# The last output projection of an encoder trunk: weight slices and four mixed blocks loaded one block earlier, slice 0 split ahead of the finish, semaphore clearing behind the memsets

## What is computed

```python
def rwkv7_time_mix(...):
    ...
    _, y = lax.scan(step, jnp.zeros((bsz, H, Dh, Dh), F32), xs)
    y = jnp.moveaxis(y, 0, 1)
    mu = jnp.mean(y, axis=-1, keepdims=True)
    var = jnp.mean(jnp.square(y - mu), axis=-1, keepdims=True)
    y = ((y - mu) * lax.rsqrt(var + RWKV_GN_EPS)).reshape(bsz, T, W) * ln_w + ln_b
    bonus = jnp.sum(rh * kh * r_k, axis=-1, keepdims=True) * vh
    return y + bonus.reshape(bsz, T, W)

def odd_layer(...):
    ...
    o_c = g_a * jax.nn.sigmoid(g_b) * jax.nn.silu(z_c.astype(F32))
    ...
    o_d = o_d * jax.nn.silu(z_d.astype(F32))
    mixed = jnp.concatenate([o_c, o_d], axis=-1).astype(x.dtype)
    return x + mixed @ w_out
```

## Time and profile before

| | us |
|---|---|
| median of 3 runs | 1481.3 |
| lowest and highest | 1479.28, 1483.59 |
| the profiled execution | 1474.99 |
| its span, first to last instruction | 1473.2 |

### The profile page before, as it was taken

One profiled execution on the slowest core, in us unless ns is written; L12 is line 12 of the kernel. 1 busy time (PEld: TensorE's weight loads), 2 busy tenths in 40 slices (PEclk: granted clock), 3 DMA queues, 4 the chain that ended last, 5 costly groups with the idle time before them and its releaser, 6 DMA issues. The chain is left out here.

```text
span 1473.2 us, 20646 instructions
## 1 busy us (share of the span) xinstructions
PE 1285.9 (87%) x8498; PEld 1069.1 (73%) x8498; DVE 892.4 (61%) x1191; ACT 481.5 (33%) x823; POOL 306.1 (21%) x156
## 2 busy tenths in 40 slices
PE   4999999979879959987997999999942788899698
PEld 4677888868568947876886888887721677889587
DVE  5267763840067646237978456686969888364831
ACT  5233344321336643223242212225462312222400
POOL 2223221211013346013131112122400400000420
PEclk9999999989989979998999999999965699999899
DMA  5212211320310012431242341621200000000523
GB/s 190 44 44 54 47 44 51 111 87 15 115 50 1 1 67 91 157 86 44 87 118 85 82 107 30 193 58 39 77 15 0 2 1 2 22 37 2 201 85 114
DMA packets 117558, 97.79 MB, mean 66 GB/s; under 512 B 37016, under 2 KB 102680, under 8 KB 117336
## 3 DMA queue, kind: packets, MB, share of 16 engines
q1 hardware_dynamic: 103832, 77.45, 17.7%
q10 hardware_dynamic: 13632, 19.01, 4.0%
HBM read 70.23 MB, written 24.51 MB: 64 GB/s over the span
## 5 line engine op out<-in xcount | busy, mean ns | idle before, releaser
L172 PE MATMUL banks<-xt_lo,w_hi 128*128 128x512 f32 x816 | 323.7, 397 | 5.9 <-POOL w_lo L521 5.9
L173 PE MATMUL banks<-xt_hi,w_lo 128*128 128x512 f32 x816 | 320.1, 392 | 0.0
L174 PE MATMUL banks<-xt_hi,w_hi 128*128 128x512 f32 x816 | 319.9, 392 | 0.0
L521 POOL TENSOR_TENSOR w_lo<-features,w_hi 128x1024 fp32r<-128x1024 f32 x55 | 148.8, 2707 | 524.2 <-ACT w_hi L531 524.2
L172 PEld LDWEIGHTS banks<-xt_lo,w_hi 128*128 128x128 f32 x816 | 154.8, 190 | 41.7 <-POOL w_lo L521 6.2
L174 PEld LDWEIGHTS banks<-xt_hi,w_hi 128*128 128x128 f32 x816 | 154.6, 190 | 32.7
L173 PEld LDWEIGHTS banks<-xt_hi,w_lo 128*128 128x128 f32 x816 | 154.8, 190 | 31.5
L580 ACT ACTIVATE temporaries<-banks 128x1024 f32<-128x1024 f32 x47 | 56.0, 1192 | 328.6 <-PE banks L174 320.7
L172 PE MATMUL banks<-xt_lo,oout_mh 128*128 128x512 f32 x128 | 51.1, 400 | 11.9 <-DVE xt_lo L1609 11.9
L300 PE MATMUL banks<-temporaries,features 128*128 128x128 f32 x256 | 37.8, 311 | 25.9 <-DVE temporaries L277 25.9
L531 ACT ACTIVATE w_hi<-features 128x1024 fp32r<-128x1024 f32 x55 | 57.8, 1054 | 1.6 <-PEq L197 1.0
(11 more groups left out here) (488 smaller groups left out, 2602.0 us busy)
## 6 DMA issues: line engine op xcount, KB each, us to landing
features<-in_even_w_in SPq DMA_DIRECT2D x26, 512.0 KB, 4.0
features<-in_odd_w_in SPq DMA_DIRECT2D x25, 512.0 KB, 4.5
features<-in_x SPq DMA_DIRECT2D x8, 512.0 KB, 8.0
even_gates<-temporaries ACTq DMA_DIRECT2D x8, 512.0 KB, 2.6
features<-even_gates SPq DMA_DIRECT2D x8, 512.0 KB, 8.8
features<-in_even_w_out SPq DMA_DIRECT2D x8, 512.0 KB, 3.5
temporaries<-in_x SPq DMA_DIRECT2D x8, 512.0 KB, 4.5
h_between_layers<-features SPq DMA_DIRECT2D x8, 512.0 KB, 2.9
```

Source lines behind the costliest of these rows:

```text
L172: nc.tensor.matmul(out, w[0], x[1], start=start, stop=False)
L173: nc.tensor.matmul(out, w[1], x[0], start=False, stop=False)
L174: return nc.tensor.matmul(out, w[0], x[0], start=False, stop=stop)
L521: nc.gpsimd.tensor_tensor(wl[n % 2], wr[n % NW], wh[n % 2].bitcast(F32), ALU.subtract).then_inc(low, 1)
```

## The change

Four things are changed, all in the odd layer.

- The loads of the first three weight slices and of S5's four blocks move from the beginning of block 4 to block 3, behind the gate loads in SyncE's queue. S5's blocks get other places in SBUF (`s5_out`), since their old ones are in use in block 3. Two of these places are later written by the high parts `mh[4]`, `mh[5]` and one by the low part of a weight slice; hence the two new waits on `low_m`.
- In block 4 the due numbers of the early slices change: on ScalarE from 5, 7.5, 10, 12.5 to 0, 2.5, 5, 7.2; on GpSimd from 5 + 2.5k to 2.5k; on VectorE from 6, 9.5, 11, 15.5 to -1, 6, 11, 15.5; on PE from 8, 11.5, 15, 18.5 to 1, 6, 9.5, 14. The finish's numbers stay.
- The clearing of blocks 1 to 3 is due at 4 instead of -2.
- `fetch` and its loop are gone from `project_out`; it is given the semaphores `mixed_in` instead.

```diff
@@ project_out
     def scalar(act):
         for k in range(KT):
-            yield 5 + 2.5 * k if k < early else base + k
-            if k < len(fetch):
+            yield (0, 2.5, 5, 7.2)[k] if k < early < KT else base + k
+            if k < len(mixed_in):
                 act.wait_ge(mixed_in[k], 16)
             if k == early:
                 act.wait_ge(*ready)
+                act.wait_ge(low_m, early)
...
     def gpsimd(pool):
         for k in range(KT):
-            yield 5 + 2.5 * k if k < early else base + k
+            yield 2.5 * k if k < early else base + k
...
         for k in range(KT):
-            yield 8 + 3.5 * k if k < early else base + 2 + k
+            yield (1, 6, 9.5, 14)[k] if k < early < KT else base + 2 + k
...
     def vector(dve):
         for k in range(KT):
-            yield (6, 9.5, 11, 15.5)[k] if k < early < KT else base + k
+            yield (-1, 6, 11, 15.5)[k] if k < early < KT else base + k
+            if k == early:
+                dve.wait_ge(low_m, early)
@@ gates_of
+        for to, what, sem in ahead:
+            sp.dma_start(to, what).then_inc(sem, 16)
         sp.wait_ge(gates_in, 16 * 4)
@@ odd_layer
-    side_by_side(co, clearing(co), invert(co, "ri0", first.n_st, R7_INVERT[0]), r7_prepare(co, second, beside_preparation(33)))
-    side_by_side(co, clearing(co), r7_state(co, first), invert(co, "ri1", second.n_st, R7_INVERT[1], pace=lambda t: 1.5 * t))
-    side_by_side(co, clearing(co), gates_of(co, zg), r7_state(co, second), r7_finish(co, first, (co.gates_in, 64), A_BIG, 0, lambda t: 5 + 3.4 * t))
+    side_by_side(co, clearing(co, at=4), invert(co, "ri0", first.n_st, R7_INVERT[0]), r7_prepare(co, second, beside_preparation(33)))
+    side_by_side(co, clearing(co, at=4), r7_state(co, first), invert(co, "ri1", second.n_st, R7_INVERT[1], pace=lambda t: 1.5 * t))
+    w_in, mixed_in = ([co.sem(f"oout_{n}{i}", kept=True) for i in range(count)] for n, count in (("w", 3), ("mixed", WB)))
+    s5_out = [co.at(at, (T,)) for at in (A_F[3], A_F[3] + 1024, A_BIG + 14336, A_BIG + 15360)]
+    loads = [(co.at(A_F[4] + 1024 * i, (D,)), a["odd_w_out"][0][i * P:(i + 1) * P, :], w_in[i]) for i in range(3)]
+    loads = [load for i in range(WB) for load in loads[i:i + 1] + [(s5_out[i], oc[i], mixed_in[i])]]
+    side_by_side(co, clearing(co, at=4), gates_of(co, zg, loads), r7_state(co, second), r7_finish(co, first, (co.gates_in, 64), A_BIG, 0, lambda t: 5 + 3.4 * t))
     side_by_side(co, clearing(co, at=100), r7_finish(co, second, None, A_BIG + 4096, 6, lambda t: t),
-                 project_out(co, "oout", a["odd_w_out"][0], zc + r, [A_F[2] + 1024 * k for k in range(KT)], [A_F[0] + 1024 * k for k in range(KT)], x, dst,
-                             co.output_stored, fetch=[(zc[b], oc[b]) for b in range(WB)], early=WB, ready=(co.finish_done, 2)))
+                 project_out(co, "oout", a["odd_w_out"][0], s5_out + r, [A_F[2] + 1024 * k for k in range(KT)], [A_F[0] + 1024 * k for k in range(KT)], x, dst,
+                             co.output_stored, fetched=w_in, early=WB, ready=(co.finish_done, 2), mixed_in=mixed_in))
```

More of the change, by code:

```diff
@@ L1502, in swa_attend, with project_out @@
     return dict(sync=sync, gpsimd=gpsimd, tensor=tensor, vector=vector, scalar=scalar)
-def project_out(co, tag, w, mixed, hi_at, lo_at, res, dst, stored, fetched=False, fetch=(), early=KT, ready=None, keep=None):
+def project_out(co, tag, w, mixed, hi_at, lo_at, res, dst, stored, fetched=False, early=KT, ready=None, keep=None, mixed_in=()):
     nc = co.nc
@@ L1519, in project_out @@
     resin = [co.sem(f"{tag}_r{i}") for i in range(3)]
-    mixed_in = [co.sem(f"{tag}_mixed_in{i}") for i in range(len(fetch))]
     high_w, high_m, low_w, low_m, multiplied, added = (
@@ L1533, in sync @@
                 sp.dma_start(wr[k], w[k * P:(k + 1) * P, :]).then_inc(loaded[k], 16)
-            if k < len(fetch):
-                sp.dma_start(*fetch[k]).then_inc(mixed_in[k], 16)
-        for k in range(3, len(fetch)):
-            sp.dma_start(*fetch[k]).then_inc(mixed_in[k], 16)
         for k in range(3):
@@ L2604, in r7_state, with gates_of @@
     return dict(gpsimd=gpsimd, tensor=tensor, vector=vector, scalar=scalar)
-def gates_of(co, gates):
+def gates_of(co, gates, ahead):
     gates_in = co.sem("r7_gates_in")
```

1 line of the change is left out of this document (removed).

## The result

| | before | after |
|---|---|---|
| median of 4 runs | 1481.16 us | 1506.34 us |
| lowest and highest | 1479.28, 1483.59 | 1493.44, 1513.67 |
| ratio of the times (95%) | | 1.0156 (1.0125 to 1.0187) |
| the profiled execution, its span | 1474.99, 1473.2 | 1493.44, 1491.7 |
| mean granted clock in it | 0.930 | 0.929 |

Slower, as forecast, but by 25 us and not by 9. The time lies 15.8 us above the forecast and 10 us above the range. The profiled execution took 1493.44 us, 2.9 more than the forecast; the other three of the four took 1502.9 to 1513.7 us. A ratio leaves out the runs that lie more than 1.5% above the fastest of their kernel, and the medians here don't, so where many runs are long the ratio is lower than the medians give. There are two questions: whether the walk through the kernel was right, and what the longer executions are.

What follows compares the result with a forecast made beforehand. It took VectorE's start in the first inversion block and the last block's VectorE and PE chains as bounding; -5.4 + 14.6 + 0 = +9.2 us gives 1484.2, plus 6.3 carried over 1490.5 us, range 1482 to 1496.

Steps and rivals of the forecast that it cites:

- Clearing, -5.4 us: First inversion block: GpSimd's two memsets go ahead of 90 clears, so VectorE's next instruction starts 5.4 us earlier.
- Loads, 0: Second state block: seven 512 KB loads moved there cost 0 to 1.4 us, taken as 0.
- The walk through block 4: Last block, walked engine by engine in the new order: it grows by 13.3 to 15.9 us, middle 14.6.
- half a fall of the clock: Last block, PE's 3.7 us wait for `ready`: last matmul at 1482.0, or 1484.6 with a third fall; half taken.
- GpSimd's hold-up to L2643: Last block, VectorE's finish: the subtraction is held up 2.2 us by GpSimd's third pass.
- The sum, +9.2 us: Whole kernel: -5.4 for the first inversion block, +14.6 for the last block, 0 for the rest.
- the sentence on the two state blocks: Both state blocks: the same clearing move, with 48 and 30 clears, is off the path, 0 gained, 0 lost.
- rival C: Last block's waits as forecast, but the clearing in the first inversion block gains nothing: 1496 to 1497 us; chance 0.07.
- the difference is carried over unchanged: Whole run: the median's 6.3 us above the profiled execution is kept, taking 1484.2 to 1490.5 us.
- A: Last block's waits come but are cheap, +4.5 to +10.0 there: 1480.4 to 1485.9 us, no measurable change; chance 0.13.
- B: Last block: PE is not held up and keeps its 6.2 us earlier start: 1469.7 us; chance 0.05.

Runs made afterwards that it cites:

- early_splits: Changed kernel with early-slice due numbers -1, -0.5, 3, 11 on VectorE and 1, 6, 9.5, 15.5 on PE: 1472.43 us, ratio 0.9927; again 1477.65 us, 0.995.
- new_order: Changed kernel with early-slice due numbers 1, 6, 11, 15.5 on PE and 3, 6, 11, 12 on VectorE: 1475.97 us, ratio 0.9958.
- clear_only: Kernel before with only the clearing moved behind the memsets: 1474.43 us, ratio 0.9958; again 1491.57 us, ratio 1.0022.

## Why the prediction was right in its sum and wrong in its time

**Clearing, -5.4 us: right for block 1.** -4.9 to -5.1 in every trace with the move but the last of early_splits, where it was -3.95. From the transpose to L802 the gain is 5.48 us (7.60 before, 2.12 after); the 0.5 are lost behind it. The memset beside the transpose took 0.95 us and the transpose 2.09, as alone before, so these two cost each other nothing. The Trainium skill (SBUF — State Buffer, Who interferes with whom) has it that a VectorE instruction with at most one SBUF input does not contend with GpSimd outside VectorE's two-port modes; the transpose has one input, and for it and the memset this trace agrees. What the section says of VectorE's two-input instructions, which the prediction cites, is not tried by this pair.

**Loads, 0: right for the time of the state blocks** (188.62 against 188.59), and right that ScalarE is free to begin.

**The walk through block 4: right, step by step.** The measured times less the 2.75 us by which the block starts later:

| | walked | measured |
|---|---|---|
| first projection matmul | 1370.4 | 1370.56 |
| PE's wait for slice 1 | 6.1 | 6.24 |
| slice 1's split done | 1383.1 | 1383.1 |
| first transposes done | 1394.9 | 1395.2 |
| PE's wait for slice 3 | 4.9 | 5.0 |
| second transposes done | 1407.5 | 1408.1 |
| `ready` | 1411.2 | 1411.9 |
| PE's wait for `ready` | 3.7 | 3.82 |
| last matmul done | 1482.0 to 1484.6 | 1484.6 |

I took half a fall of the clock, 1.3 us, for the third wait. It fell, 0.8 us after PE had gone on, and eight matmuls from 1415.46 to 1418.87 stood 0.43 us apart instead of 0.23, which is 1.6 us. With the 0.7 by which `ready` came later than walked, that is 1.0 of the 1.1 us between 14.6 and 15.7. One thing was in the wrong place: I gave GpSimd's hold-up to L2643, and it fell on L2641, the 128x32 scaling, which took 2.38 us:

```profile
1375.39 2.38 DVE L2641 TENSOR_SCALAR constants<-constants 128x32 f32<-128x32 f32 x1
1377.80 2.29 DVE L2643 TENSOR_TENSOR features<-features,constants 128x2048 f32<-128x2048 f32 x1
```

The sum is the same, since the same pass of GpSimd lay in the way. It did matter in new_order, where I went wrong by such a place.

**The sum, +9.2 us: measured +10.7** (-5.0 + 15.7), in the changed stages. In the runs that are not long it is less: the 14 of the changed kernel have a median of 1488.7 us, those of before 1481.6, 7.1 us apart. The median of all 21 is 1490.5, the number that was forecast, but this is luck: it mixes two groups, of which the forecast knew one.

**The step that failed** is the sentence on the two state blocks: "It is off the path: 0 gained, 0 lost." By the rows it was so, and in a short execution it is so. But it holds a second claim, that blocks with the same instructions take the same time in all executions. They take 188.6 or 210.8, and long executions were more frequent with the move; the term that the prediction put at 0 for the state blocks is 18 to 22 us in a long execution. Three of the first four executions of the changed kernel were long, so their median, 1506.34, is a long execution's time. That these three lost it in the state blocks too is inferred from the five traces with 206.7 to 210.9: of the first four the one kept trace is that of the short run. Where a third is long, three or more of four are long about one time in nine (4 x 1/27 x 2/3 + 1/81); so the first measurement overstates the loss, and the 1.0107 and 1.0062 of the repeats are nearer to it. The range had no case for it: rival C, the highest, ended at 1497.

**A second step was weak**: "the difference is carried over unchanged". The 6.3 us by which the median lay above it were taken for a constant. The profiled execution of before (1474.99) is among the shortest: its 99 other runs go from 1474.2 to 1496.5, with one at 1577.1, and have a median of 1482.2. Besides, what lies ahead of the change made 7.7 us between the two profiled executions. So two single profiles can't be compared by their ends; their stages can, to 0.1 us for the most part and to about 1 where the clock's falls lie differently.

**The rivals.** A (waits come, but cheap) falls: all three falls of the clock came, and filling PE's idle time gave back 3.9 to 5.0 us. B (PE not held up) falls for this order; its condition, slice 1's split at PE when slice 0 ends, is met in early_splits, and even there the last block gains 0.7 us, not 6.2. C (the clearing gains nothing) falls as it was put, since the mechanism was to be in block 1; but what came is of its kind, a loss that goes with the clearing, in another block.

## What to carry to other kernels

Where one engine feeds two consumers, an early start of one of them is paid for by the order behind it. Here PE's early products waited for splits that stood behind five steps of the finish, and the finish's transposes stood behind those products; two numbers of PE's order were worth 14.1 us, while the start, 6.1 us earlier, was worth 0.7 at best. Walk both chains to the point where they meet, with the order of each engine, before you move one.

A stage measured from landmark to landmark mostly repeats to 0.1 us, and where it doesn't, as the state blocks here, the difference can be read from the granted clock; a whole execution doesn't repeat: take some ten runs, look at whether they fall into groups, and compare the stages of a short and of a long one before you believe that a change far away costs nothing.

## What was not expected of the hardware

- The same program runs the state blocks in 188.6 us at a mean granted clock of 0.95 in one execution, and in 210.9 us at 0.82 in another (clear_only, clear_only_again). PE isn't idle there: in 70 us it has 64.4 us of busy time with 772 matmuls in the one, and 66.3 us with 650 in the other, at 0.61. The Trainium skill (TensorE: Matmul & The Clock Gate, Part 1) says that the number of half-clock matmuls at a start differs from run to run and that this is below one percent of a typical span. Here it is a stretch in the middle of the program, of which that sentence does not speak, and the difference is 22.3 us, 1.5% of the span.
- An instruction of 128x32 elements, 0.18 us when alone (in early_splits_again), took 2.38 us beside a low part of GpSimd, that is until the pass had ended. The Trainium skill (SBUF — State Buffer, Who interferes with whom) counts such a scaling among the operations that can take the shared ports, and says that the later one is fully blocked; the trace agrees, and how small the blocked instruction is doesn't matter.
- Where VectorE and GpSimd both have a row of such instructions, they took turns in the order of their starting: 1.0, 2.1 and 2.0 us were lost by three VectorE instructions in a row in new_order. What a hold-up costs hangs on how the ends fall, to 2 us each.
